# Softmax attention with the values stationary for two heads at once, denominators from GpSimd's sums, and a last norm in token halves: one Trainium2 core

## What is computed

```
q = axial_rope(rms_norm(q.reshape(b, s, 16, 64), q_norm_w), ...)
k = axial_rope(rms_norm(k.reshape(b, s, 4, 64), k_norm_w), ...)
sc = jnp.einsum("bqgrd,bkgd->bgrqk", q, k) * 64 ** -0.5      # 16 heads, no mask
p = jax.nn.softmax(sc, axis=-1)
attn = jnp.einsum("bgrqk,bkgd->bqgrd", p, v)
...
x = x + mla_layer(...)
return x * rsqrt(mean(x * x, axis=-1) + EPS) * final_norm
```

## Time and profile before

| | |
|---|---|
| median of 3 runs | 1614.25 us (1612.87 to 1616.03) |
| the profiled execution | 1610.29 us, its span 1608.5 us |
| TensorE busy | 1574.3 us, 98% of the span |
| its weight loads | 1292.2 us, 80% |
| VectorE busy | 982.3 us, 61% |
| ScalarE busy | 762.0 us, 47% |
| GpSimd busy | 794.1 us, 49% |

### The profile page before, as it was taken

The page is one execution under the profiler, slowest core; times in us unless marked ns, Lnnn a source line. Parts: engine busy times, 40 slices in busy tenths (PEclk is TensorE's granted clock), DMA queues, the critical chain, the costliest instruction groups (busy, mean ns, idle before and its releaser), DMA issues. The chain is left out here.

```text
span 1608.5 us, 23675 instructions
## 1 busy us (share of the span) xinstructions
PE 1574.3 (98%) x8199; PEld 1292.2 (80%) x8199; DVE 982.3 (61%) x1316; ACT 762.0 (47%) x1389; POOL 794.1 (49%) x578
## 2 busy tenths in 40 slices
PE   7999999999999999999999999999999999999997
PEld 4778888888788789887878888888888878777876
DVE  4898888888559797587261321212278865557662
ACT  4675666676534644323343332324467645433432
POOL 1556666566646420256744444444644556334424
PEclk9999999999999999999999999999999999999998
DMA  8434443433322200467423333333332333221202
GB/s 318 128 121 122 131 119 111 138 116 115 110 86 74 59 27 1 143 237 254 159 77 100 92 105 92 102 95 92 98 92 81 99 104 105 67 59 53 66 21 91
DMA packets 76389, 171.29 MB, mean 106 GB/s; under 512 B 8256, under 2 KB 8640, under 8 KB 72832
## 3 DMA queue, kind: packets, MB, share of 16 engines
q1 hardware_dynamic: 68976, 133.09, 28.4%
q10 hardware_dynamic: 7312, 36.83, 6.6%
HBM read 167.67 MB, written 2.23 MB: 106 GB/s over the span
## 5 line engine op out<-in xcount | busy, mean ns | idle before, releaser
L606 POOL TENSOR_TENSOR w_lo<-w_raw,w_hi 128x512 fp32r<-128x512 f32 x455 | 661.8, 1476 | 554.4 <-ACT w_hi L654 553.8
L1175 PE MATMUL bank<-a_hi,w_hi 128*128 128x512 f32 x984 | 390.6, 397 | 2.3 <-ACT gates_early L719 1.2
L1177 PE MATMUL bank<-a_hi,w_lo 128*128 128x512 f32 x984 | 383.7, 390 | 0.0
L1176 PE MATMUL bank<-a_lo,w_hi 128*128 128x512 f32 x984 | 383.1, 389 | 0.0
L654 ACT ACTIVATE w_hi<-w_raw 128x512 fp32r<-128x512 f32 x457 | 263.9, 621 | 161.7 <-PE bank L1196 126.8
L1175 PEld LDWEIGHTS bank<-a_hi,w_hi 128*128 128x128 f32 x984 | 184.9, 188 | 44.0 <-issue 3.6
L1177 PEld LDWEIGHTS bank<-a_hi,w_lo 128*128 128x128 f32 x984 | 184.7, 188 | 39.5
L1176 PEld LDWEIGHTS bank<-a_lo,w_hi 128*128 128x128 f32 x984 | 185.0, 188 | 39.1 <-issue 1.9
L1193 PE MATMUL bank<-b_hi,w_hi 128*128 128x512 f32 x536 | 210.7, 393 | 3.0 <-DVE y_full L2356 1.8
L1196 PE MATMUL bank<-b_lo,w_hi 128*128 128x512 f32 x536 | 208.8, 390 | 0.0
L1194 PE MATMUL bank<-b_hi,w_lo 128*128 128x512 f32 x536 | 208.7, 389 | 0.0
(11 more groups left out here) (382 smaller groups left out, 2625.3 us busy)
## 6 DMA issues: line engine op xcount, KB each, us to landing
w_raw<-ws SPq DMA_DIRECT2D x457, 256.0 KB, 2.7
cs_rows<-cs_scratch ACTq DMA_DIRECT2D x16, 1024.0 KB, 5.3
ada_piece<-ada ACTq DMA_DIRECT2D x16, 1024.0 KB, 5.5
ada_piece<-ada SPq DMA_DIRECT2D x8, 1024.0 KB, 16.9
x_stream<-x SPq DMA_DIRECT2D x2, 1024.0 KB, 6.8
x_stream<-x ACTq DMA_DIRECT2D x1, 2048.0 KB, 8.1
out<-x_stream SPq DMA_DIRECT2D x8, 256.0 KB, 2.2
rope_table<-rope ACTq DMA_DIRECT2D x1, 512.0 KB, 3.4
```

The costliest lines, as they stand in the source:

```text
L606: nc.gpsimd.tensor_tensor(wlo[b][:, :], raw[n % RAW_RING][:, :], r32(whi[b][:, :]), ALU.subtract)\
L1175: mm(out, lh, rh, start=first, stop=False)
L1176: mm(out, lh, rl, start=False, stop=False)
L1177: return mm(out, ll, rh, start=False, stop=last)
```

## The change

In words, part by part:

1. `values(u, c)` now serves a pair of heads. The 64 values of a chunk are stationary, and 512 columns of probabilities move: one matmul for each head, the first head's output on partitions 0 to 63 and the second's on 64 to 127 of one bank. All four chunks of both heads stand in the odd head. The output lies feature by token at once. The odd heads' probabilities go to a second buffer (`probs_odd`, from pair 4 on q_full).
2. The denominators: GpSimd adds the four chunks of probabilities of each head (`add_chunks`, three adds of 128x512) into sq0 or sq1, and in the next even head TensorE sums both over keys with one moving column (`take_sums`, 8 matmuls), VectorE inverts them and spreads each over 64 columns of tmp4 or tmp5 (`invert_sums`), TensorE turns that in the odd head (`turn_inverse`, four transposes in the place of `turn_pair`), ScalarE copies it back (`keep_inverse`), and VectorE scales the pair in its bank (`scale_pair`). `share` is gone. `round_pair` and `split_pair` read the pair's bank, and come one head and two heads later.
3. The two casts of a query go from VectorE to ScalarE (`query_high`), ahead of `max_row(h + 1)` in ScalarE's list; VectorE keeps the subtraction (`query_low`).
4. In an even head `row_of_max(h + 1)` is the last thing before `scores(h + 1)`.
5. GpSimd's `add_chunks` of all heads stand behind the last w_lo slabs of the stage, and the last rotation behind `add_chunks(5)`.
6. The last norm: the tiles ("ob", 6) and ("ob", 7) are computed in two halves of 256 tokens each, every weight block twice, and the norm of the first half (sums, root, rows, scaling, stores of two tiles each) stands beside the second half's matmuls. The root's table is loaded ahead of the ("ob", m).

```diff
+            def add_chunks(h):
+                probs, out, at = probs_of(h), sq[h % 2], ADDED_AT + (NCH - 1) * h
...
+                pool.wait_ge(exp_done, NCH * h + 2)
+                if h >= 2:
+                    pool.wait_ge(sums_taken, SCANNED + h // 2)
+                nc.gpsimd.tensor_tensor(out[:, :], probs[:, 0, :], probs[:, 1, :], ALU.add).then_inc(chunks_added, 1)
+                for c in range(2, NCH):
...
+                    nc.gpsimd.tensor_tensor(out[:, :], out[:, :], probs[:, c, :], ALU.add).then_inc(chunks_added, 1)
...
+                for rows in (own, other):
+                    A(qHH[b][rows, :], qF[own, u, :], ACT.Copy).then_inc(q_high, 1)
...
                 if h == 0:
                     gate_early(("ga", EARLY_IN_QK[QK[-1]]))
-                if h % 2 == 0 and h:
-                    round_pair(h // 2 - 1)
+                if h % 2 and u:
+                    keep_inverse(u - 1)
+                if h + Q_RING - 1 < N_Q:
+                    query_high(h + Q_RING - 1)
                 if h + 1 < N_Q:
                     max_row(h + 1)
+                if h % 2 and u:
+                    round_pair(u - 1)
...
+            def values(u, c):
+                pe.wait_ge(exp_done, NCH * (2 * u + 1) + c + 1)
+                if c == 0 and u >= 2:
+                    pe.wait_ge(rdyB, PAIRS + u - 1)
+                for hh in range(2):
+                    ins = mm(OQ[u % 2][hh * HD:(hh + 1) * HD, :], vv[:, c, u // 2, :], probs_of(2 * u + hh)[:, c, :],
+                             start=(c == 0), stop=(c == NCH - 1))
+                ins.then_inc(pv_done, 1)
+
+            def take_sums(u):
+                pe.wait_ge(chunks_added, ADDED_AT + (NCH - 1) * 2 * (u + 1))
...
+                for hh in range(2):
+                    for i in range(NCH):
+                        ins = mm(SUMS[:, 2 * i + hh:2 * i + hh + 1], sq[hh][:, i * P:(i + 1) * P], ones[:, 0:1], start=True, stop=True)
+                ins.then_inc(sums_taken, 1)
...
+                if h % 2 == 0:
+                    if h:
+                        take_sums(h // 2 - 1)
+                    row_of_max(h + 1)
+                    continue
...
+                    turn_inverse(u - 1)
                 for c in range(NCH):
-                    values(h, c)
+                    values(u, c)
                     if c == 1 and h + 1 < N_Q:
                         row_of_max(h + 1)
+            take_sums(QT - 1)
...
+                if h % 2 and u:
+                    scale_pair(u - 1)
+                if h % 2 == 0 and u >= 2:
+                    split_pair(u - 2)
                 if h + Q_RING - 1 < N_Q:
-                    split_q(h + Q_RING - 1)
-                if h % 2 == 0 and h:
-                    split_pair(h // 2 - 1)
-                share(h)
+                    query_low(h + Q_RING - 1)
+                if h % 2 == 0 and u:
+                    invert_sums(u - 1)
...
+            half_tile(("ob", KT - 2), 0, lambda: None)
+            half_tile(("ob", KT - 1), 0, lambda: half_stat(0, KT - 2))
+            half_tile(("ob", KT - 2), 1, lambda: half_stat(0, KT - 1))
+            half_rows(0)
+            half_tile(("ob", KT - 1), 1, lambda: half_stat(1, KT - 2))
+            half_stat(1, KT - 1)
+            half_rows(1)
```

More of the change, by code:

```diff
@@ L360, in build @@
                 qL = [sb(f"q_lo{b}", [HD + 1, SEQ], F32R) for b in range(Q_RING)]
[L361 removed]
+                vv = sb("v_by_token", [P, NCH, N_KV, HD])
                 PT = sb("probs", [P, NCH, SEQ])
[L363 removed]
                 qF = sb("q_full", [P, QT, SEQ])
@@ L511, in _ @@
                 sp.dma_start(raw[s % RAW_RING][:, :], d["ws"][s]).then_inc(w_in[s % RAW_RING], 16)
-            for m in range(KT):
-                sp.wait_ge(fin_ready, m + 1)
-                sp.dma_start(d["out"][m], xF[:, m, :]).then_inc(s_out, 16)
-            sp.wait_ge(s_out, 16 * KT)
+            out = d["out"].rearrange("k p n -> p k n")
+            for half, step in ((0, 2), (1, 1)):
+                w = token_half(half)
+                for m in range(0, KT, step):
+                    sp.wait_ge(fin_ready, half * KT + m + step)
+                    sp.dma_start(out[:, m:m + step, w], xF[:, m:m + step, w]).then_inc(s_out, 16)
+            sp.wait_ge(s_out, 16 * (KT + KT // 2))
         @block.gpsimd
@@ L520, in fill_attention @@
             def fill_attention():
-                parts = [(vv[:, :, :, HD:HD + 1], 1.0)]
-                parts += [(r32(kH[g][HD:HD + 1, :]), 1.0) for g in range(N_KV)]
+                parts = [(r32(kH[g][HD:HD + 1, :]), 1.0) for g in range(N_KV)]
                 for n, (part, value) in enumerate(parts):
@@ L620, in _ @@
                     add_probs(h)
+                if s == summed_at:
+                    for h in range(N_Q):
+                        add_chunks(h)
+                        if h == 5:
+                            rotate(QK[-1])
                 if s == fill_at:
@@ L1145, in _ @@
             round_head(N_HEADS - 1)
-            for m in range(KT):
+            A(small[:, 81:82], eps, ACT.Sqrt)
+            for m in range(KT - 2):
                 hi_upto(slab_of(("ob", m)) + AHEAD)
@@ L1149, in _ @@
                 square("fin", m, xF[:, m, :])
-            root("fin", 1.0 / D_MODEL)
+            hi_upto(N_SLABS - 1)
+            for half in range(2):
+                w = token_half(half)
+                for m in (KT - 2, KT - 1):
+                    b, used = BANK_OF[("ob", m)]
+                    act.wait_ge(evac[b], used + 1 + half)
+                    n = STAT_AT["fin"][0] + m
+                    if half == 0:
+                        act.wait_ge(sq_added, SQ_USED[n - 2][1])
+                    A(sq[n % 2][:, w], xF[:, m, w], ACT.Square).then_inc(sq_ready, 1)
+                act.wait_ge(stat_mm, SUM_AT["fin"] + 2 * half)
+                A(roots_of_half(half), HALF_SUMS[half][:, 0:NCH // 2], ACT.Sqrt, bias=eps, scale=1.0 / D_MODEL)\
+                    .then_inc(std_ready, 1)
         @block.tensor
```

219 lines of the change are left out of this document (153 added, 66 removed).

## The result

| | before | changed |
|---|---|---|
| median of the runs | 1614.25 us (1612.87 to 1618.15, 5 runs) | **1627.63 us** (1624.01 to 1628.72, 5 runs) |
| ratio, with its 95% interval | | 1.0086 (1.0075 to 1.0096) |
| profiled execution | 1610.29, span 1608.5 | 1628.6, span 1626.6 |
| mean granted clock of TensorE | .996 | .987 |
| first scores of the attention | 538.31 | 540.59 |

Slower by 13.4 us where 5.9 were forecast. TensorE is still busy for 97% of the span (1583.4 of 1626.6 us), so the busy shares tell nothing. The clock does (the clock that TensorE was granted, as a share of full speed). All five runs line up with it: 1624.01 us at a mean clock of .991, 1625.83 at .990, 1627.63 at .988, 1628.72 at .988, 1628.6 at .987.

What follows compares the result with a forecast made beforehand. TensorE bound the kernel, with VectorE a hair behind in the attention. Terms -4.4 + 3.3 + 1.7 + 5.2 + .7 - .4 - .2 = +5.9 us on 1614.25 gave 1620.2 us, range 1611 to 1626.

Steps and rivals of the forecast that it cites:

- TensorE's stream: Attention: paired values save, column sums, width changes and the bare row cost; TensorE alone nets -4.4 us.
- Far from 13.6: Sign of being wrong: pair period of heads 10 to 13 far from 13.6 us, the stream alone.
- Head 0, ScalarE: Slabs, gate copy and query copies ahead of `max_row(1)` keep head 1's scores where they were: +3.3 us.
- Head 2, GpSimd: TensorE waits in head 2 for sums after GpSimd's late slabs and six additions: +1.7 us.
- VectorE in heads 5, 7 and 9: Third score tiles wait for VectorE's maximum, its instructions held by GpSimd's additions: +1.4, +2.4, +1.4, together +5.2 us.
- Head 15: `take_sums(7)` waits for GpSimd's six additions begun in head 14: +.7 us.
- The end: Final norm in halves: dearer 256-column passes and sums against a shorter chain and scalings: -.2 us, bounds -1 and +1.5.
- The clock: Rival: TensorE's clock falls after near-idle even-head stretches, up to 1.7 us each; one to four falls, 1621.9 to 1627, chance .2.
- My own sign for a sum too low: If the profile's clock row shows .5 inside the attention, the forecast sum is too low.

Runs made afterwards that it cites:

- the kernel of ratio 1.0031 with the row between the sums: Changed kernel, row's transposes between two heads' sums, spreading copy on ScalarE, row earlier there, VectorE's last half inverses and rotations in odd heads: 1617.78 us, ratio 1.0031.
- the kernel with the old norm: Changed kernel with the final norm as before, in whole tiles, and the attention as changed: 1626.07 us, ratio 1.0090.
- without the additions: Changed kernel with five unread matmuls per even head from head 2, and GpSimd's 48 additions on one column instead of 512: 1615.28 us, ratio 1.0017.
- the norm alone: Kernel before with the final norm in token halves and nothing else: 1610.92 us, ratio .9994.
- with fills: Changed kernel with five unread 384-column matmuls behind the row's transposes in each even head from head 2: 1618.80 us, ratio 1.0043.
- with the row between the sums: Changed kernel with the row's transposes between the two heads' sums, no unread matmuls: 1630.26 us, ratio 1.0114.
- with ScalarE's copy: Changed kernel with five unread matmuls per even head from head 2, and the inverse sums' spreading copy on ScalarE instead of VectorE: 1618.39 us, ratio 1.0034.
- the kernel with fills in waits alone: Ratio 1.0051 kernel (heads 1, 2 relieved) plus five unread matmuls ahead of head 2's row, two behind each of head 15's last three score tiles: 1618.92 us, ratio 1.0032.
- the kernel with the last sums in the tile behind: Ratio 1.0016 kernel (three more unread matmuls per even head), last pair's sums moved into the middle of the tile after the attention: 1613.54 us, ratio 1.0005.

## Why the prediction was wrong

The direction held, the size did not: the time lies outside the range. The step that failed is the clock, which the sum had at nothing. By its own steps, each for the attention of the profiled executions, which lost 137.44 - 124.02 = 13.4 us against 6.1 forecast (the sum's 5.9 without the end's -.2):

- **TensorE's stream** held. Values side by side, sums, row and width changes each measured within .1 us; the full-clock pair is 13.74 for 13.6. Over seven pairs that is +1.0. "Far from 13.6" was the test for being wrong here, and it isn't.
- **Head 0, ScalarE** held: 13.74 instead of 13.54, forecast -.1. So +.3.
- **Head 2, GpSimd**, +1.7: not seen. Head 1 ran 8.87 us where 7.2 were forecast, 1.7 longer, most of it by the slow step at 554.78, and that gave GpSimd the time it lacked. It is real where head 1 runs at a full clock: in the kernel of ratio 1.0031 with the row between the sums the first sums start 1.40 after the start of the last score tile instead of some .3, so 1.1 late.
- **VectorE in heads 5, 7 and 9**, +5.2: +1.1 in the changed kernel, in head 9 alone. In heads 5 and 7 the slow clock made TensorE late instead. In the kernel with the old norm, heads 6 and 7 had a full clock and the late maximum, 14.74 us. With the clock kept the three cost 1.1, 1.0 and 1.1. The mechanism was right (without the additions all went), its size was too large, most of all in head 7 (2.4): I let each held instruction wait out a whole addition, but the subtraction's middle value was .92.
- **Head 15**, +.7: .53 of idle before the sums, a start-to-start gap of 1.12 for .43, so .7. Right.
- **The end**, -.2: .25 less by the trace of the norm alone, 0 to -1 by the runs. Right.
- **The clock** was the step that failed. I made it a rival of one to four falls, chance .2, and left it out of the sum. There were eight steps in the attention, in six places. Their price is the staircase, 1.48: 11.9 us, taken for all eight though it was read from the pairs. What I had from rows 12, a fall behind an idle TensorE, pointed the right way but was too narrow, since falls came behind stretches without a wait as well (last section). I had written down thin stretches of 3.1 us in every even head and the waits of head 0, and didn't count them: seven and one. Each is a candidate; the forecast's count was a guess below that number, without a run behind it. My own sign for a sum too low, .5 of the clock inside the attention, is what the profile shows.

Together 6.1 + 1.0 + .3 - 1.7 - 4.1 + 11.9 = 13.5, for 13.4 measured. The falls hid some 4 us of the very waits of which the sum consisted (1.7 in head 2, 2.1 in heads 5 and 7), so their net price was nearer 8 us than 11.9, and the two can't be priced apart: for a TensorE that is itself late, nobody is late. The number of steps isn't fixed by the code either: the kernel with the old norm had six with the same attention.

Of the 18.1 us between the two profiled spans 13.4 are these. Another 2.3 lie ahead of the attention (540.59 against 538.31), where the two kernels do the same. There the startup of the changed kernel had the clock at .50 from 15.5 to 22.3 us, that of the one before from 54.2 to 57.6, and the profiled runs of later experiments started the attention between 538.2 and 544.4. The remaining 2.4 lie behind it, which is the last section's last point.

## What to carry to other kernels

Here a stretch in which TensorE moved almost nothing was priced twice: by its own length, and by what the clock did behind it. Count such stretches before a change, one possible fall for each, and look at where the added ones stand. When a wait is in the way and can't be removed, matmuls whose result nothing reads can be worth more than they take, as they were here; but moving work to an idle engine puts a wait into that engine's queue, and everything behind it is late.

## What the runs showed of the hardware

Two matmuls of 512 columns with 64 stationary columns each, on different halves of the output partitions, start .01 us apart and take .43 a pass together, as the mixer's do at 128 columns.

In all six kernels whose head 1 starts 2.7 us after head 0's row (the changed one, those with the old norm, with fills, with the row between the sums, without additions, and with ScalarE's copy) the clock goes to .50 within .7 us of that start. In the changed kernel each of the six places where it fell lies within 1 us of an odd head's first scores, or of the start of the tile behind the last sums: what TensorE did before was one-column sums, the row and a wait, for head 1 the row and the wait alone, for the tile a wait and the sums alone. It is not shown why heads 8, 12 and 14, with the same instructions, had none.

A wait isn't needed for a fall. These are TensorE's rows at the end of head 10 in the kernel with fills in waits alone, one right behind the other without a wait, and the window of the slow step that follows:

```profile
620.11 0.95 PE L1633 MATMUL bank<-consts,sq 128*128 128x1 f32 x8
621.06 0.65 PE L1600 MATMUL bank<-consts,small 128*128 128x128 f32 x4
621.54 0.95 PE L1633 MATMUL bank<-consts,sq 128*128 128x1 f32 x8
622.38 0.57 PE L1612 MATMUL bank<-q_hi_twice,k_hi_over_lo 128*128 128x512 f32 x1
```

```profile
622.65:626.06 3.41, 3.41 (x9) 2.69 (x9) 1.47 (x3) 2.12 (x5) 3.12 (x3) 0.50 0.00 0
```

Nor did the sums bring one every time: in the first kernel with fills, where only the wait behind them is filled, no fall came from head 4 on.

Behind the attention the changed kernel loses another 2.4 us where its code is the same, .9 of it up to about 1002 us of the kernel before and 1.6 from there on. ScalarE's rows at two places of the expert and second-attention stages, of the kernel before:

```profile
1002.25 0.60 ACT L948 ACTIVATE tmp<-bank 128x512 f32<-128x512 f32 x1 [3.14 <-PE bank L1177]
...
1557.96 0.63 ACT L1109 ACTIVATE a_hi<-tmp 128x512 fp32r<-128x512 f32 x1 [6.68 <-DVE tmp L2578]
```

and of the changed kernel:

```profile
1018.81 0.60 ACT L1018 ACTIVATE tmp<-bank 128x512 f32<-128x512 f32 x1 [3.14 <-PE bank L1260]
...
1576.11 0.63 ACT L1179 ACTIVATE a_hi<-tmp 128x512 fp32r<-128x512 f32 x1 [6.68 <-DVE tmp L2731]
```

557.30 - 555.71 = 1.6 us, without a wait that is new. The kernels that have the changed attention all show 1.4 to 1.6, the one with the norm alone .2. The new attention also changes where buffers lie in SBUF (`b_lo` is in two parts with `probs_odd` between them, `v_by_token` is narrower). One part of the loss can be placed: the matmuls that read `c_hi` and `c_lo`, at a full clock, take 48.0 us from the first start to the last of those with `c_hi` and `w_hi` where they took 46.8 before, 47.1 with the norm alone and 47.6 with the last sums in the tile behind, and those of `c_hi` with `w_lo` have a middle duration of 396 ns (398 with the last sums in the tile behind) for 388 before and with the norm alone. So it is TensorE's own pace that is slower there. Whether the place of the buffers is the cause wasn't tried; it stays open. It is what keeps the kernel with the last sums in the tile behind from being even: of the 1.9 us between its span (1610.4) and that of the kernel before, .1 lies ahead of the attention, .1 in it and 1.7 behind it.
